# Order of the four matmuls in one step of the gate and up units of a two-layer hybrid block

## The reference

```python
D_MODEL = 1024
SEQ = 256
DEPTH = 2
D_FF = 2816

def swiglu_ffn(h, w_gu, w_down):
    g, u = jnp.split(h @ w_gu, 2, axis=-1)
    return (jax.nn.silu(g) * u) @ w_down

for l in range(DEPTH):
    x = x + 0.5 * swiglu_ffn(rms_norm(x, ffn1_norm[l]), ffn1_w_gu[l], ffn1_w_down[l])
    ...
    x = x + 0.5 * swiglu_ffn(rms_norm(x, ffn2_norm[l]), ffn2_w_gu[l], ffn2_w_down[l])
```

## Time and profile before

| what | value |
|---|---|
| median of 3 runs | 1392.82 us (1392.22 to 1393.33) |
| the profiled execution's own time | 1393.32 us |
| its span | 1389.6 us |
| granted TensorE clock, mean | 0.993 |
| PE busy | 1352.4 us (97%) |
| DVE busy | 956.6 us (69%) |
| ACT busy | 784.0 us (56%) |
| wide matmuls, line 1670 | 1408 |
| short matmuls, line 1674 | 1408 |

### The profile page before, as it was taken

One profiled execution on the slowest core, in us unless ns is written; L12 is line 12 of the kernel. 1 busy time (PEld: TensorE's weight loads), 2 busy tenths in 40 slices (PEclk: granted clock), 3 DMA queues, 4 the chain that ended last, 5 costly groups with the idle time before them and its releaser, 6 DMA issues.

```text
span 1389.6 us, 23738 instructions
## 1 busy us (share of the span) xinstructions
PE 1352.4 (97%) x8778; PEld 1203.1 (87%) x8778; DVE 956.6 (69%) x1484; ACT 784.0 (56%) x1392; POOL 149.9 (11%) x219
## 2 busy tenths in 40 slices
PE   6999998999999999999999999999999999999997
PEld 6888888998989988888888888899888989888886
DVE  5766677877766667666676666778877656676665
ACT  5555555755654566555555555576556446655554
POOL 3010011022410110000010000100224001100000
PEclk9999999999999999999999999999999999999999
DMA  8677656555445537666566667455454554466661
GB/s 232 206 205 212 186 172 177 176 159 166 138 153 191 174 94 219 197 187 193 172 187 201 185 181 214 139 179 182 138 171 135 169 182 152 132 206 196 192 183 74
DMA packets 286384, 243.36 MB, mean 175 GB/s; under 512 B 14345, under 2 KB 263609, under 8 KB 286305
## 3 DMA queue, kind: packets, MB, share of 16 engines
q1 hardware_dynamic: 284176, 236.77, 56.3%
q10 hardware_dynamic: 1600, 4.25, 0.9%
q0 software_dynamic: 528, 1.26, 0.6%
HBM read 241.18 MB, written 1.27 MB: 174 GB/s over the span
## 4 chain that ended last, share of the span: by engine, by line
issue 63%; PE 24%; DVE 4%; POOLq 2%; POOL 2%; ACT 2%; DVEq 1%; DMA 1%; SPq 0%; ACTq 0%
PE work L1592 15%; PE work L1670 3%; DVE w_lo L521 2%; PE work L1674 1%; PE acc L1629 1%; PE acc L1825 1%; POOL diag L727 1%; POOLq L726 1%; ACT w_hi L513 1%; PE work L1835 1%; POOLq L723 1%; PE work L1815 1%; POOLq L721 1%; PE work L1801 0%; DVE act L1145 0%
## 5 line engine op out<-in xcount | busy, mean ns | idle before, releaser
L521 DVE TENSOR_TENSOR w_lo<-raw,w_hi 128x1024 fp32r<-128x1024 f32 x444 | 545.8, 1250 | 85.1 <-ACT w_hi L513 83.5
L513 ACT ACTIVATE w_hi<-raw 128x1024 fp32r<-128x1024 f32 (+1 forms) x442 | 450.3, 1051 | 25.1 <-PE acc L1629 25.1
L1670 PE MATMUL work<-act,w_hi 128*128 128x512 f32 x1408 | 441.9, 395 | 4.5 <-DVE w_lo L521 4.5
L1674 PEld LDWEIGHTS work<-act,w_lo 128*128 128x128 f32 x1408 | 265.8, 189 | 60.6
L1592 PE MATMUL work<-act,w_hi 128*128 128x256 f32 x1536 | 278.6, 282 | 3.4 <-DVE merged L1259 1.9
L1674 PE MATMUL work<-act,w_lo 128*128 128x256 f32 x1408 | 278.7, 279 | 0.0
L1592 PEld LDWEIGHTS work<-act,w_hi 128*128 128x128 f32 x1536 | 237.7, 190 | 9.4 <-issue 4.2
L1670 PEld LDWEIGHTS work<-act,w_hi 128*128 128x128 f32 x1408 | 215.7, 189 | 7.7 <-issue 4.7
L1592 PE MATMUL work<-act,w_lo 128*128 128x256 f32 x768 | 214.1, 279 | 0.0
L834 ACT ACTIVATE gu_s<-work 128x256 f32<-128x256 f32 x176 | 57.9, 381 | 189.3 <-PE work L1674 189.3
L1180 DVE TENSOR_TENSOR gu_s<-gu_s,work 128x256 f32<-128x256 f32 x176 | 66.1, 417 | 122.6 <-ACT gu_s L834 122.6
(11 more groups left out here) (245 smaller groups left out, 1827.9 us busy)
## 6 DMA issues: line engine op xcount, KB each, us to landing
raw<-in_ffn_w_gu SPq DMA_DIRECT2D x174, 512.0 KB, 5.0
raw<-in_w_in SPq DMA_DIRECT2D x52, 1024.0 KB, 5.2
raw<-in_ffn_w_down SPq DMA_DIRECT2D x44, 1024.0 KB, 5.0
raw<-in_w_branch SPq DMA_DIRECT2D x12, 1024.0 KB, 5.0
raw<-in_w_mkv SPq DMA_DIRECT2D x8, 1024.0 KB, 5.4
raw<-in_w_out SPq DMA_DIRECT2D x8, 1024.0 KB, 4.9
raw<-in_w_mq SPq DMA_DIRECT2D x4, 1024.0 KB, 5.3
raw<-in_w_mo SPq DMA_DIRECT2D x4, 1024.0 KB, 5.1
```

The source lines that it names most:

```text
L513: eng.activation(halves(w_hi, slot, kind, part), halves(raw, slot, kind, part), ACT.Copy)\
L521: eng.tensor_tensor(halves(w_lo, slot, kind, part), halves(raw, slot, kind, part), halves(w_hi, slot, kind, part).bitcast(F32), ALU.subtra ...
L1670: pe.matmul(work[:, 2 * c + g, :], w_hi[:, slot, at_w:at_w + P], act[:, :, k, :], start=(k == 0), stop=False, skip_group_check=True)
L1674: mm = pe.matmul(work[:, 2 * c + g, 0:SEQ], w_lo[:, slot, at_w:at_w + P], act_hi[:, k, :], start=False, stop=(k == KT - 1), skip_group_che ...
```

## The change

Within each step, the short matmul of a sum comes right behind the wide one of the same sum. The order becomes wide 0, short 0, wide 1, short 1. Nothing else is changed: same operands, same flags, same waits, same number of instructions.

```diff
@@ -1669,8 +1669,6 @@
                             at_w = k * 256 + g * P
                             pe.matmul(work[:, 2 * c + g, :], w_hi[:, slot, at_w:at_w + P], act[:, :, k, :],
                                       start=(k == 0), stop=False, skip_group_check=True)
-                        for g in range(2):
-                            at_w = k * 256 + g * P
                             mm = pe.matmul(work[:, 2 * c + g, 0:SEQ], w_lo[:, slot, at_w:at_w + P], act_hi[:, k, :],
                                            start=False, stop=(k == KT - 1), skip_group_check=True)
                             if k == KT - 1:
```

## The result

The changed kernel takes 1401.78 us (median of 4, 1401.60 to 1403.26) against 1393.07 of the kernel before, measured beside it: a ratio of 1.0054, 95% interval 1.0040 to 1.0068. (A ratio on record is not exactly the quotient of the two medians, which is 1.0063 here.) It is slower by more than half a per cent, 8.7 us by the medians, where 3.5 us less was forecast, and it lies outside the range. The profiled execution took 1401.60 us with a span of 1399.1; that of before had 1389.6. 9.5 us are to be found.

A forecast was written before the change was run, and what follows sets the result against it. PE's back-to-back matmul stream was taken as the bound. A step falling from 693 to 688 ns, 5 ns times 700, gave 3.5 us off the 1392.82 us median: 1389.3 us, range 1382.0 to 1397.0.

The forecast's parts named there:

- What bounds the kernel: In the four feed-forward networks, PE's own matmul stream is the bound; PE is busy for 97% of the span.
- the unit's head and end: At a gate and up unit's first and last matmuls, the swap was to cost and gain nothing.
- the bank: A short matmul adding into columns the wide one has just written was to cost nothing by itself.
- The two levels and their price: Gate and up matmul spacings: short 113 ns (256 columns) or 226 (512), long 118 and 236, 4.4% more.
- all at the long spacing, 708 ns: Upper bound for a gate and up step: 15 ns above 693, or 10.5 us more over 700 steps.
- reading (a): In gate and up steps, the matmul ahead sets the spacing: 688 ns a step, 3.5 us less; chance 0.34.
- Reading (b): In gate and up steps, a `w_lo` load under a matmul lengthens it: 698 ns a step; chance 0.16.
- Reading (c): A rhythm of column and load streams settles by how a unit begins, then holds; step between 678 and 708 ns.
- both bounds: Gate and up step with every matmul at short spacing, 678 ns, or long, 708: 10.5 us to either side.
- the locked long spacing: Rival: gate and up steps stay at the long spacing throughout, 10.5 us more, 1403.3 us; chance 0.07.
- What would show it: Expected profile: wide durations near 388, short near 281, units 5.50 us, down units and line 1592 keeping their levels.
- rival 2: Slower: `w_lo` loads under both wide matmuls add 5 ns a step, 3.5 us more, 1396.3 us; chance 0.16.

The follow-up runs named there:

- the mirrored order: Kernel before with each gate and up step ordered wide 0, wide 1, short 1, short 0, except step 7 of a unit; ratio 1.0007.
- the alternation across banks: Kernel before reordered to wide 1 (k), short 0 (k), wide 0 (k+1), short 1 (k), each short behind the other bank's wide; ratio 1.0063.
- the gate split run: Changed kernel with the gate's wide matmul made as two of 256 columns, the up's left whole; 1402.42 us (before 1393.21).
- the pair at the head: Kernel before with step 0 of each gate and up unit whole, wide matmuls of steps 1 to 7 split into two of 256; 1380.33 us, ratio 0.9931.

## Why the prediction was wrong

- *What bounds the kernel* was right: PE's stream, with nothing to hide a ns of it. No wait was added and none went; ACT's 81 idle stretches still end with the unit's last matmul (197.3 us where the earlier trace rows had 189.3, for the units are longer). The accounts of the unit's head and end, and of the bank, came out as said; the mirrored order and the alternation across banks show the bank directly.
- *The two levels and their price* were right: 113 and 118, 226 and 236, and durations as a measure of spacings. (One quotient is slightly off, 1.76 us over fifteen spacings is 117.3 and not 117.5; nothing changes by it.) The bound "all at the long spacing, 708 ns" is what came, at 706, and 10.5 us to that side against 9.5 of the span.
- *The step that failed* is the choice of reading (a), that the level of a matmul is set by the one ahead of it. It rested on one step with four matmuls and on the earlier trace rows, and gave 2 x (226 + 118) = 688 ns for the new step; the step took 706. In the new order a wide one behind a short one takes 235, not 226, while the short one behind a wide one takes 118, as read. What 226 needs is more than a short one in front, and in the gate split run even four don't give it.
- *Reading (b)* has the wide ones right (235) and the short ones wrong (118 for 113). The run with all short ones last puts `w_lo` loads under small ones at 276.
- *Reading (c)*, a rhythm that settles and then holds, was what the two units of the earlier trace rows had shown: the same 48 instructions at either level. It was named and left out of the sum because the trace can't say where a new order settles. It should have had the greatest weight, and with it both bounds the greatest chance; 0.07 for the locked long spacing was far too little. A row that shows the same code at two levels says that no rule by neighbours can be whole.
- *What would show it* had the down units and line 1592 keep their levels. The down units did; the stretch of line 1629 in the mixing stage did not, and cost 0.8 us, but it changes without regard to the edit.
- *The range* ended below the measured time for the same reason. The point from which rival 2 was to decide (a wide one behind a short one above 231) was reached, yet by another mechanism and at nearly three times its price.

What stays open is the cause below the rule. The lock over whole networks would fit two streams, moving columns and stationary columns, that meet in one of two alignments; that is a guess, and no run here shows it. Nor is it known what in the hand-over from a split down unit defeats the pair.

The Trainium skill, on the page TensorE: Matmul & The Clock Gate, section Back-to-back issue gap, gives N/2.4 + 2.5 ns for an isolated warm matmul of N columns; the estimate by it for 256 columns is 109 ns, whatever stands around it. The traces do not agree: the same width took 113 or 118 in the same code.

## What to carry to other kernels

Where PE is the bound and its matmuls are back to back, compare the durations of the same line in different units: two values 5 or 10 ns apart (276 and 281, 388 and 398) mean that order and width of neighbours matter, in either direction: here 0.5% lost by order alone, 0.7% won with the pair at the head. Don't alternate 512 and 256 columns one by one in a stream like this one; keep wide ones together, or split them to one width and see by the trace, network by network, at which level the stream has locked. A change of order can't be priced from the rows of another order: give both bounds a real chance, and measure.

## What the runs showed of the hardware

More matmuls and more weight loads took less time. Six of 256 columns with six loads took 680 ns where four of 512 and 256 with four loads took 693 or 706 for the same products. And the level is a state of the stream, not of the instruction: in one execution whole networks of the same code ran at 113 or 118 ns a matmul, and in two of the kernels the down units behind spoiled gate and up units ran at 398 ns, though nobody had touched their code; in the changed kernel they stayed at 388 to 394. So what stands ahead can move the level of untouched code, but the runs do not give the rule by which it does.
